# A tuned four-layer transformer kernel on one core: the order of evictions, silus and splits in the first two layers, and of output chunks in the two mix layers

## The reference, cut to what matters

```python
# first block: layer a (dilated attention), layer b (grouped-query attention)
for i in range(2):
    h = rmsnorm(x, norm_g[i]); mem_h = rmsnorm(mem, mem_norm_g[i])
    proj = h @ w_in[i]                       # q, k, v of the mixer, q_mem, gate (1536 columns)
    o_mix = mixer_dilated(...) if i == 0 else mixer_axial_gqa(...)
    o_mem = memory_attention(q_mem, mem_h, w_mem_kv[i], ...)   # heads of 128, rms norm of q and k
    x = x + (concat([o_mix, o_mem]) * silu(gate)) @ w_out[i]
# second block: two "mix" layers
for l in range(2):
    h = x @ w_in_2[l]
    mix = concat([sliding_window_sink_attn(...), indexer_sparse_attn(...), mla_attn(...)])
    x = layer_norm(alpha * x + mix @ w_out_2[l])
    x = layer_norm(alpha * x + moe_ffn(x))   # 16 experts, the router picks two of one group
```

## Time and profile before

| | |
|---|---|
| three timed runs | 1187.78, 1190.66, 1190.87 us, median 1190.66 us |
| the profiled execution | 1184.36 us |
| its span, first to last instruction | 1182.9 us |
| TensorE busy | 1121.7 us, 95% |
| VectorE busy | 895.0 us, 76% |
| ScalarE busy | 740.4 us, 63% |
| HBM | 219.13 MB read, 186 GB/s over the span |
| mean granted TensorE clock | 0.990 |

### The profile page before, as it was taken

The page is one execution under the profiler, slowest core; times in us unless marked ns, Lnnn a source line. Parts: engine busy times, 40 slices in busy tenths (PEclk is TensorE's granted clock), DMA queues, the critical chain, the costliest instruction groups (busy, mean ns, idle before and its releaser), DMA issues.

```text
span 1182.9 us, 14669 instructions
## 1 busy us (share of the span) xinstructions
PE 1121.7 (95%) x5515; PEld 918.5 (78%) x5515; DVE 895.0 (76%) x1462; ACT 740.4 (63%) x1313; POOL 0.2 (0%) x4
## 2 busy tenths in 40 slices
PE   7899999999998899999999999999989989999996
PEld 5688887788777788887788787877778878787774
DVE  4756757677667876775668768999986876899996
ACT  5645665655646665556356456888846655688883
POOL 0000000000000000000000000000000000000000
PEclk9999999999999999998999999999999999999998
DMA  9554454453432464631543224999936332499991
GB/s 291 194 212 142 143 178 140 146 177 107 143 132 83 153 225 156 224 107 49 201 146 131 98 90 143 350 359 364 360 111 203 127 102 91 143 348 357 364 351 40
DMA packets 131841, 221.25 MB, mean 187 GB/s; under 512 B 6144, under 2 KB 77360, under 8 KB 131760
## 3 DMA queue, kind: packets, MB, share of 16 engines
q1 hardware_dynamic: 127920, 213.21, 52.2%
q10 hardware_dynamic: 3840, 6.98, 1.8%
HBM read 219.13 MB, written 1.05 MB: 186 GB/s over the span
## 4 chain that ended last, share of the span: by engine, by line
PE 74%; DVE 13%; ACT 8%; issue 3%; DMA 2%; ACTq 0%; DVEq 0%
PE bank L487 20%; PE bank L489 20%; PE bank L488 20%; PE bank L849 3%; PE bank L784 2%; DVE wL L440 2%; ACT wH L432 2%; ACT S L804 2%; PE bank L636 1%; DMA ring<-in_w_mem_kv 1%; DVE mx L793 1%; PE bank L2271 1%; PE bank L830 1%; PE bank L2320 1%; PE bank L1726 1%
## 5 line engine op out<-in xcount | busy, mean ns | idle before, releaser
L440 DVE TENSOR_TENSOR wL<-ring,wH 128x1024 fp32r<-128x1024 f32 (+1 forms) x316 | 375.7, 1213 | 148.0 <-ACT wH L432 147.0
L432 ACT ACTIVATE wH<-ring 128x1024 fp32r<-128x1024 f32 (+1 forms) x316 | 320.6, 1047 | 32.8 <-PE bank L489 16.6
L487 PE MATMUL bank<-wH,hTH 128*128 128x512 f32 (+2 forms) x592 | 238.8, 403 | 4.8 <-DVE wL L440 2.5
L488 PE MATMUL bank<-wL,hTH 128*128 128x512 f32 (+2 forms) x592 | 233.1, 394 | 0.0
L489 PE MATMUL bank<-wH,hTL 128*128 128x512 f32 (+2 forms) x592 | 233.0, 394 | 0.0
L487 PEld LDWEIGHTS bank<-wH,hTH 128*128 128x128 f32 x592 | 112.3, 190 | 29.6 <-DVE wL L440 3.5
L489 PEld LDWEIGHTS bank<-wH,hTL 128*128 128x128 f32 x592 | 112.1, 189 | 24.7
L488 PEld LDWEIGHTS bank<-wL,hTH 128*128 128x128 f32 x592 | 112.3, 190 | 22.9 <-issue 0.5
L487 PE MATMUL bank<-wH,xgH 128*128 128x512 f32 x256 | 104.8, 409 | 0.0
L488 PE MATMUL bank<-wL,xgH 128*128 128x512 f32 x256 | 101.3, 396 | 0.0
L489 PE MATMUL bank<-wH,xgL 128*128 128x512 f32 x256 | 101.3, 396 | 0.0
(11 more groups left out here) (297 smaller groups left out, 1869.2 us busy)
## 6 DMA issues: line engine op xcount, KB each, us to landing
ring<-in_w_in_a SPq DMA_DIRECT2D x44, 1024.0 KB, 4.9
ring<-in_w_out SPq DMA_DIRECT2D x20, 1024.0 KB, 4.8
ring<-in_w_down SPq DMA_DIRECT2D x20, 1024.0 KB, 6.4
ring<-in_w_gate SPq DMA_DIRECT2D x36, 512.0 KB, 5.2
ring<-in_w_up SPq DMA_DIRECT2D x36, 512.0 KB, 6.5
ring<-in_w_in_b SPq DMA_DIRECT2D x14, 1024.0 KB, 5.0
ring<-in_w_mem_kv SPq DMA_DIRECT2D x8, 1024.0 KB, 7.0
ring<-in_w_in SPq DMA_DIRECT2D x8, 1024.0 KB, 5.4
```

The source lines that it names most:

```text
L432: act.e.activation(quarter_parts(q)[0], quarter_in_ring(q), COPY).then_inc(w_high, 1)
L440: dve.e.tensor_tensor(lo, quarter_in_ring(q), hi.bitcast(F32), SUB).then_inc(w_low, 1)
L487: pe.e.matmul(o, a[0], b[0], start=first, stop=False)
L488: pe.e.matmul(o, a[0], b[1], start=False, stop=False)
```

## The change

The work is the same; its order on the three engines differs.

- Start of layer a: four quarters instead of two are taken before the memory keys are turned, on TensorE and ScalarE. On VectorE one quarter's cut goes between the two multiplies of the memory keys' norm (`amid`), one behind it. Only the tables of group 0 are made there; those of groups 1 and 2 are made in `between(2)` of u=0 and u=1.
- Layer a, u=2: the last quarter's cut on VectorE goes ahead of the silu in `between(3)`.
- Layer a, u=4: VectorE's cuts go from the even `between` (ahead of emit) to the odd ones (behind it).
- Layer a, u=5: ScalarE takes the last quarter of g02 and its eviction ahead of the y chunks of part 0; it does silu passes 0 and 1 before `act_flip(qT)` and pass 2 right behind. VectorE does silu and gating ahead of two cuts instead of behind them. TensorE takes its quarters in the run at `between` 0, 2, 3 instead of 0, 2, 4.
- Layer b, units: the y chunks of part 2 are brought out at the start of `between(6)` (ScalarE) and `between(7)` (VectorE), ahead of a quarter's cut and the eviction of g11; the passes of silu g10 go from `between` 6, 7, 8 to 8, 8, 9.
- Layer b, end: VectorE adds tile 0, brings out the low parts of the turned X tile 0, and then adds tile 1.
- Mix layers: the y chunks are turned in `between(5)` and `between(9)`, behind the values of units 1 and 3 and ahead of the scores of units 3 and 5, on all three engines.

```diff
-        def dve_out(label):
+        def dve_out(label, tiles=range(2)):
             dve.wait_ge((d_x, 16))
-            for i in range(2):
+            for i in tiles:
...
             if gain is not None:
+                if amid:
+                    amid()
                 dve.wait_ge((d_rows, 112))
...  pe_layer_a
-            pe_ahead(2)
+            pe_ahead(4)
             pe_flip(("mKT", 0), chunk(qkv[1][1]), 4, [at("heads", "mk", 0)])
...
-                    pe_run(units, lambda n: pe_ahead(1 - n % 2))
+                    pe_run(units, lambda n: pe_ahead(1 if n in (0, 2, 3) else 0))
...  act_layer_a
-            act_ahead(2)
+            act_ahead(4)
             act_flip(("mKT", 0), 4, mKT)
...
                 if u == 5:
+                    act_ahead(1)
                     act_flip_y("o0", 0, 4)
                     act_upto("o00", 4)
...
                 if u == 5:
                     act_silu("g02", 0, at("silu", "g01"))
+                    act_silu("g02", 1)
                 act_flip(("qT", u), 4, qT)
                 if u == 5:
-                    act_silu("g02", 1)
+                    act_silu("g02", 2)
                 act_ahead(2 if u == 5 else 3)
-                if u == 5:
-                    act_silu("g02", 2)
                 act_flip(("kT", u), 4, kT)
...  dve_layer_a
-            dve_head_norm(("mk", 0), qkv[1][1], gain=R("mk0"))
-            dve_ahead(2)
-            dve_tables(0, "cA", "sA", 16, ["qa0", "ka0", "qa1", "ka1", "qa2", "ka2"])
+            dve_head_norm(("mk", 0), qkv[1][1], gain=R("mk0"), amid=lambda: dve_ahead(1))
+            dve_ahead(1)
+            dve_tables(0, "cA", "sA", 16, ["qa0", "ka0"])
...
+                if u == 5:
+                    dve_silu("g02")
+                    dve_gated("o0", 2)
                 dve_ahead(2 if u == 5 else 3)
...
-                    dve_run(units + mem_units(0), lambda n: dve_ahead(1 - n % 2))
+                    both_kinds = units + mem_units(0)
+                    dve_run(both_kinds, lambda n: dve_ahead(1 if n % 2 or n == 2 * len(both_kinds) else 0))
                     dve_to("a52")
                 elif u == 5:
-                    dve_silu("g02")
-                    dve_gated("o0", 2)
...
                         dve_ahead(1 - n % 2)
+                        if u < 2 and n == 2:
+                            dve_tables(2 * u + 2, "cA", "sA", 16, [f"qa{u + 1}", f"ka{u + 1}"])
+                        if u == 2 and n == 3:
+                            dve_ahead(1)
...  act_layer_b
             def between(n):
+                if n == 6:
+                    act_flip_y("o1", 0, 4)
                 act_ahead(1)
...
-                if n == 6:
+                if n == 7:
+                    act_ahead(1)
+                if n == 8:
                     act_silu("g10", 0, at("silu", "g12"))
-                if n == 7:
-                    act_flip_y("o1", 0, 4)
-                    act_ahead(1)
-                    act_silu("g10", 1)
-                if n == 8:
                     act_to("g11")
                     act_upto("o12", 4)
+                    act_silu("g10", 1)
+                if n == 9:
                     act_silu("g10", 2)
...  dve_layer_b
+                if n == 7:
+                    dve_flip_y("o1", 0, 4)
                 dve_ahead(1 if n in (0, 1, 9, 12) else 2)
...
-                    dve_flip_y("o1", 0, 4)
...
-            dve_out("o1")
+            dve_out("o1", [0])
+            dve_flip_x(0, 0)
+            dve_out("o1", [1])
...  mix layers (TensorE; ScalarE and VectorE alike)
-        OUT_AT = {3: (0, 2, 2), 5: (2, 2, 4)}
+        OUT_AT = {5: (0, 2, 2), 9: (2, 2, 4)}
...
-            def behind_scores(n):
-                if n in OUT_AT:
-                    outputs(*OUT_AT[n])
-                    pe_upto(f"p{l}0", OUT_AT[n][2] + 2)
...              in between(n), at its end
+                if n in OUT_AT:
+                    outputs(*OUT_AT[n])
+                    pe_upto(f"p{l}0", OUT_AT[n][2] + 2)
```

More of the change, by code:

```diff
@@ L718, in act_head_norm, with dve_head_norm @@
             act_ahead(2 if rope else 1)
-        def dve_head_norm(key, buf, n=4, gain=None, idx=None, half=None, off=0):
+        def dve_head_norm(key, buf, n=4, gain=None, idx=None, half=None, off=0, amid=None):
             w = n * P
@@ L1776, in between @@
                     flip_one(("kS", l), lambda i: HR[:, i, 896:1024], at("sparse", l))
-            pe_run(others, between, behind_scores)
+                if n in OUT_AT:
+                    outputs(*OUT_AT[n])
+                    pe_upto(f"p{l}0", OUT_AT[n][2] + 2)
+            pe_run(others, between)
             pe_out_last_two(f"p{l}", lambda i, d: last_outputs(1) if (i, d) == (0, 1) else None)
@@ L1866, in act_mix_layer @@
             act_upto(f"p{l}0", 2)
-            def behind_scores(n):
-                if n in OUT_AT:
-                    act_flip_y(f"p{l}", OUT_AT[n][2], 2)
-                    act_upto(f"p{l}0", OUT_AT[n][2] + 2)
             def between(n):
@@ L1880, in between @@
                     act_flip(("kS", l), 1, kI)
-            act_run(others, between, behind_scores)
+                if n in OUT_AT:
+                    act_flip_y(f"p{l}", OUT_AT[n][2], 2)
+                    act_upto(f"p{l}0", OUT_AT[n][2] + 2)
+            act_run(others, between)
             act_flip_y_tile(f"p{l}", 6, 1)
@@ L1900, in dve_mix_layer @@
         def dve_mix_layer(l):
-            if l == 0:
-                dve_flip_x(0, 0)
             dve_cut(start(f"h{l}0") + 4)
@@ L1991, in behind_scores @@
             def behind_scores(n):
-                if n in OUT_AT:
-                    dve_flip_y(f"p{l}", OUT_AT[n][2], 2)
-                    dve_upto(f"p{l}0", OUT_AT[n][2] + 2)
                 if n == 0:
@@ L2009, in between @@
                     dve_ahead(1)
+                if n in OUT_AT:
+                    dve_flip_y(f"p{l}", OUT_AT[n][2], 2)
+                    dve_upto(f"p{l}0", OUT_AT[n][2] + 2)
             dve_run(others, between, behind_scores)
```

## The result

The changed kernel took 1167.91 us (median of 4 runs, 1166.48 to 1174.45) against 1189.22 us for the kernel before (4 runs). The ratio of the two is 0.9857, 95% interval 0.9822 to 0.9892; measured again, in five rounds with others, 0.9869 (0.9844 to 0.9895). So it is faster, by 1.3 to 1.4%. Ratio and median differ because the forecast starts from 1190.66 us: the kernel before, in 29 later executions beside the experiments, had a median of 1184.77 us (1181.36 to 1190.40), close to its profiled execution (1184.36). From that one the forecast's sum gives 1168.0, and 1167.91 was measured.

The account below looks back on a forecast made before the run. TensorE was taken as the bound, busy for 1121.7 of 1182.9 us, so an order could give back 61 us of idle time beside its clock. The terms summed to 16.4 us: 1190.7 - 16.4 = 1174.3 us, range 1169 to 1182.

Parts of the forecast that it names:

- Start of layer a: Memory keys' norm: stall of 3.3 us becomes 0.9 and 1.7 us of clock come back, +4.1 us.
- Tables: Table products moved into u=0 and u=1 make u=0's values 1.4 us late and cost nothing in u=1: -1.4 us.
- u=2: Layer a: TensorE's 1.19-us wait at 225.63 for a cut behind a silu ends that much earlier, +1.1 us.
- u=4: Layer a: the bank's 1.22-us wait for an emit behind a cut goes, the cuts being no later, +1.2 us.
- end of layer b: TensorE's 1.47-us wait at 589.05 for the low parts of X, behind two adds, goes: +1.5 us.
- u=5, first part: Layer a: earlier g02 eviction shortens the stall to 1.3 (+2.0), clock gives +1.6, gated chunk +0.6: +4.2 us.
- u=5, run: Layer a: values come at the same time through ScalarE's chain; waits of 1.88 and 0.40 become one of 2.3: 0.
- Layer b: Units: stalls of 2.75 and clock loss of 2.8 go, new stalls of 1.05, 0.85 and 1.5 come: +2.2 us.
- Mix layers: In each, waits of 1.07 and 1.43 for low parts go and one of 0.75 comes at `between(9)`: +1.75 us.
- Transfers, 0: Moved cuts free ring buffers within 2 us of before; the trace shows no wait for a transfer.
- The clock: Lowered stretches behind the stalls at 49, 357.9 and 537.5 come back: 1.7 + 1.6 + 2.8 = 6.1 us.
- slower: Rival, 1197 us: the ten new short stalls lower the clock, each for 2.8 us; chance 0.03.

Follow-up runs that it names:

- as tried: Changed kernel with the products of the tables of groups 1 and 2 ahead of VectorE's quarter in units 0 and 1: 1166.87 us, ratio 0.9838.
- the undone kernel: Changed kernel with VectorE's order in unit 4's run alone undone, its quarter again ahead of a unit's output: 1170.12 us, ratio 0.988.
- The undone part: Changed kernel with the part of unit 5 of layer a alone undone on TensorE, ScalarE and VectorE: 1170.45 us, ratio 0.9889.
- the other order for that chain: Changed kernel with unit 5's second half reordered: ScalarE's quarter split and weight copies earlier, VectorE's split behind the differences of the maxima: 1168.07 us, ratio 0.9851.
- the part undone: Changed kernel with the mix layers' part alone undone, chunks turned again behind the scores of units 3 and 5: 1170.99 us, ratio 0.9896.
- the filled kernel before: Kernel before, with 13 filling products ahead of each of its two 3.3-us waits: 1181.64 us, ratio 0.998 to the kernel before.

## Why the prediction was right

The sum 16.4 met 15.7 in the profile, and the ratio of the runs fits it. The stalls and the three places of the clock were read rightly, but that the sum came out this close is in part luck. The steps of the change brought 18.75 us, 2.35 more than forecast. That is mostly time outside the waits' brackets (0.4 us in each mix layer, 0.6 in u=4, 0.2 at the end of layer b) and a stall of 0.5 that did not come. The profile then lost 2.95 us to falls of the clock at the entry that no term foresaw. By its steps:

- **Start of layer a** (+4.1): right, stall, new stall and clock; confirmed alone at 3.96.
- **Tables** (-1.4): mechanism right, 1.45 of wait and 1.69 of time. Avoidable, as tried.
- **u=2** (+1.1, measured 1.24): no experiment of its own; the two traces alone say it.
- **u=4** (+1.2) was mis-sized: 1.85. The forecast priced the bracket, the wait of 1.22 us. Of the surplus, 0.2 is the split itself: the unit's eight turns run together in 1.04 us in the changed kernel, and cut in two by the wait they are groups of 0.60 and 0.66 (in the undone kernel). 0.3 more stand ahead of that unit's scores (328.01 before, 324.43 after, 3.6 apart where the stage began with 3.3), where no bracket shows a wait. The end of layer b has a surplus too (1.47 in the bracket, 1.71 in time).
- **u=5, first part** (+4.2): 4.8 alone. The stall of 0.5 for the gated chunk's low part did not come (365.78, no wait), and the stall at 350.58 is 1.16, not 1.3.
- **u=5, run** (0): right. 1.88 + 0.40 became one of 2.48; the chain of ScalarE set the values in both. The undone part shows both halves again, and the other order for that chain shows that it was the bound: 1.8 us earlier at the values.
- **Layer b** (+2.2, measured 2.45 and 2.59): right. Three stalls of 2.95 us (forecast 3.4) replaced two of 2.75, so without the clock it is a loss of 0.2 us; the matmuls between them took 2.65 us less (forecast 2.8). All of its gain is clock. The 0.6 us that the forecast saw inside the stage before and left out of its sum were rightly left out: TensorE mostly waited there.
- **Mix layers** (+1.75 each) were mis-sized: 2.25 each. The two waits of 2.50 went; the 0.84 us at unit 3 stayed as forecast, and the new one at `between(9)` is 0.61, not 0.75. That makes 1.9. The other 0.4 us lie outside the waits: between the same two instructions of the first mix layer TensorE's time outside waits is 40.96 us before, 40.57 in the changed kernel and 40.97 with the part undone, so the cost of restarts at waits comes and goes with the edit, as in u=4.
- **Transfers, 0**: right. No wait on a transfer appeared; the expert stages cost the same but for the clock.
- **The clock** is the step that was read too simply. The forecast took three lowered stretches from one profile as fixed prices (6.1 us) and everything else as free. In the fourteen profiles of this case (the two first, and twelve), the stretch behind the 3.3-us wait at 49 is lowered in 2 of 2 that have the wait idle, and in none without; that behind the 3.3 us in unit 5 in 2 of 2; that of layer b's old order in 3 of 3 (in one of them, the filled kernel before, for half as long), new order 0 of 11. These gains were real. But behind the 2.48-us wait it is lowered in 4 of 9, and at the first entry, with waits of 0.58 and 0.85, in 6 of 12. The forecast's rival "slower" was priced by such falls at the ten new stalls, and only behind the 2.48-us one did a lowered stretch ever begin; its argument against it, that 1.88 us at 385.79 cost no clock, was one draw: in the filled kernel before, the stretch behind the same 1.88 us was lowered (0.72 in 382 to 388).

Worked out from span times clock, the change is worth 1170.9 - 1157.9 = 13.0 us of waits and restarts (medians of the last rounds; in the two first profiles TensorE's idle time fell by 11.7 us). The rest of the 15.5 to 17 us is clock, and differs from execution to execution: the changed kernel ran at a mean granted clock of 0.985 to 0.996, the kernel before, in those rounds, at 0.986 to 0.993. The median lies under the range while the ratio doesn't because of the base of 1190.66 us. Its three runs have no recorded clock, so that they ran at a lower one than the 29 later executions is likely, not shown.

The Trainium skill, TensorE: Matmul & The Clock Gate, Part 1, states that what the chip watches runs free of the program, so that one kernel shows a different number of slow matmuls at its start from run to run. The page tells it of a kernel's start. Carried over to the middle, lowered stretches could come and go between two executions of one program, and here they did: the entry's 1.7 and 1.7 us stand in one profile of the changed kernel and not in the other.

## What to carry to other kernels

Size a stall by undoing it, or add to the bracket what the split costs the work around it: here 0.2 to 0.6 us each. Price a clock fall by how often it comes, from several profiles: compare span times granted clock to see what an edit does to waits, and the runs to see what it does to the time. Compare that product only at like clocks, since idle time in a lowered stretch enters the product at the lowered clock: one kernel, the one before, gave 1167.7 us at 0.982 and 1172.1 at 0.992. And when a step is moved ahead into an engine's order, look for where that engine only waits: the tables cost 1.7 us behind a cut and nothing ahead of it.

## What the runs showed of the hardware

- TensorE's clock goes to its lower level also where it hardly idles. In the filled kernel before, at 649 to 663 us, TensorE was busy for 13.71 of 14.00 us and ran at 0.51, in masks, score products of 64 rows by 128 or 256 columns, transposes and then quarters of a mix layer; in the 9 us ahead of it, it was busy for 8.01 and at 1.00. The same stretch of the kernel before had 1.00. Three of the fourteen profiles had such stretches. The (1 - 0.51) x 14 = 6.9 us that it costs are more than any edit of this change brings.
- A filled wait kept the clock, at both places of the one profile: 13 products on a zero vector in 3.3 us of waiting gave back 1.7 us at the first and 1.4 at the second.
- Two executions differ from the start: at 43 us, before anything that was edited, TensorE was between 0.7 us earlier and 0.8 us later than in the changed kernel's profile. Its waits there are for splits (0.30, 0.95 and 1.50 us at 33 us in three profiles); what makes them differ wasn't followed further.
